# The expert stage of a hybrid decoder step: split products of 96 columns, or plain fp32 products in three 32-column groups

## The reference

```python
def swiglu(h, wg, wu, wd):
    return (jax.nn.silu(h @ wg) * (h @ wu)) @ wd

def moe_swiglu(h, router, wg, wu, wd):
    probs = jax.nn.softmax((h @ router).astype(F32), axis=-1)
    vals, idx = lax.top_k(probs, TOP_K)
    vals = vals / jnp.sum(vals, axis=-1, keepdims=True)
    combine = jnp.sum(jax.nn.one_hot(idx, N_EXPERTS, dtype=F32) * vals[..., None], axis=-2)
    out = jnp.zeros(h.shape, F32)
    for e in range(N_EXPERTS):
        out = out + combine[..., e:e + 1] * swiglu(h, wg[e], wu[e], wd[e]).astype(F32)
    return out.astype(h.dtype)
```

## Time and profile before

| | us |
|---|---|
| median of 3 runs | 1830.04 |
| lowest and highest of them | 1827.49, 1836.27 |
| the profiled execution's own time | 1834.22 |
| its span in the profile | 1832.1 |
| first product of the expert stage starts | 840.86 |
| last product of the expert stage ends | 1804.91 |

### The profile page before, as it was taken

One profiled execution on the slowest core, in us unless ns is written; L12 is line 12 of the kernel. 1 busy time (PEld: TensorE's weight loads), 2 busy tenths in 40 slices (PEclk: granted clock), 3 DMA queues, 4 the chain that ended last, 5 costly groups with the idle time before them and its releaser, 6 DMA issues.

```text
span 1832.1 us, 24602 instructions
## 1 busy us (share of the span) xinstructions
PE 1701.7 (93%) x9755; PEld 1365.5 (75%) x9755; DVE 1331.2 (73%) x1161; ACT 1079.6 (59%) x966; POOL 133.3 (7%) x132
## 2 busy tenths in 40 slices
PE   6999989899989966778999999999999999999994
PEld 6888769899989966676777777777777777777772
DVE  5556555455457689436888889888888888888885
ACT  4445543544445422336777777777777877877773
POOL 1022210000000464001000000000000000000001
PEclk9999999899999978788999999999999999999997
DMA  8588886355453552446999999999999999999962
GB/s 318 184 265 292 299 309 239 125 184 170 158 201 139 204 165 85 180 150 229 381 354 385 373 368 379 366 382 371 355 393 368 365 384 363 388 366 359 392 241 79
DMA packets 167969, 517.81 MB, mean 283 GB/s; under 512 B 6912, under 2 KB 58312, under 8 KB 160608
## 3 DMA queue, kind: packets, MB, share of 16 engines
q1 hardware_dynamic: 146144, 446.85, 65.8%
q0 software_dynamic: 16560, 60.99, 9.6%
q10 hardware_dynamic: 5200, 9.05, 1.4%
HBM read 475.97 MB, written 40.89 MB: 282 GB/s over the span
## 4 chain that ended last, share of the span: by engine, by line
PE 85%; DVE 6%; issue 2%; ACT 2%; DMA 1%; POOL 0%; POOLq 0%; ACTq 0%; DVEq 0%
PE ps L1663 82%; PE ps L2021 1%; DVE ring L1291 1%; DVE ring L1468 1%; PE ps L1805 1%; DVE ring L1469 1%; DMA ring<-in_state_retention 1%; PE ps L1971 0%; ACT ring_low_parts L931 0%; DVE arena L1486 0%; DVE ring L1442 0%; DMA ring<-y_scr,expert_arena 0%; PE ps L2007 0%; PE ps L1725 0%; DVE ring_low_parts L1240 0%
## 5 line engine op out<-in xcount | busy, mean ns | idle before, releaser
L1615 DVE TENSOR_TENSOR ring_low_parts<-ring,expert_weights_high 128x2048 fp32r<-128x2048 f32 x336 | 761.7, 2289 | 136.1 <-ACT expert_weights_high L1105 135.3
L1105 ACT CAST expert_weights_high<-ring 128x2048 fp32r<-128x2048 f32 x336 | 639.4, 1913 | 189.7 <-PE ps L1663 184.4
L1663 PE MATMUL ps<-expert_weights_high,expert_x_parts 128*96 128x512 f32 x1792 | 453.4, 395 | 3.8 <-ACT expert_weights_high L1105 3.8
L1663 PEld LDWEIGHTS ps<-expert_weights_high,expert_x_parts 128*96 128x96 f32 x1792 | 288.6, 162 | 126.2 <-ACT expert_weights_high L1105 3.9
L1240 DVE TENSOR_TENSOR ring_low_parts<-ring,ring_low_parts 128x1024 fp32r<-128x1024 f32 (+2 forms) x180 | 214.6, 1202 | 132.1 <-ACT ring_low_parts L931 130.9
L1663 PE MATMUL ps<-normed_high,ring_low_parts 128*128 128x264 f32 x1344 | 269.6, 292 | 9.7 <-DVE normed_low L1234 9.7
L931 ACT CAST ring_low_parts<-ring 128x1024 fp32r<-128x1024 f32 (+2 forms) x180 | 179.8, 1000 | 151.1 <-PE ps L1663 151.1
L1663 PE MATMUL ps<-ring_low_parts,expert_x_parts 128*96 128x512 f32 x896 | 243.9, 394 | 0.0
L1663 PEld LDWEIGHTS ps<-normed_high,ring_low_parts 128*128 128x128 f32 x1344 | 218.9, 192 | 12.1 <-issue 10.4
L1663 PE MATMUL ps<-expert_weights_high,hide_parts 128*96 128x512 f32 x896 | 226.2, 394 | 0.0
L1663 PEld LDWEIGHTS ps<-ring_low_parts,expert_x_parts 128*96 128x96 f32 x896 | 144.5, 161 | 63.2
(11 more groups left out here) (244 smaller groups left out, 1441.0 us busy)
## 6 DMA issues: line engine op xcount, KB each, us to landing
ring<-in_moe_w_gate SPq DMA_DIRECT2D x56, 2048.0 KB, 7.7
ring<-in_moe_w_up SPq DMA_DIRECT2D x56, 2048.0 KB, 8.0
ring<-in_moe_w_down SPq DMA_DIRECT2D x56, 2048.0 KB, 7.4
ring<-in_ret_w_in SPq DMA_DIRECT2D x8, 2048.0 KB, 12.1
ring<-in_state_retention POOLq DMA_DIRECT2D x32, 512.0 KB, 7.9
out_ret_s<-ring POOLq DMA_DIRECT2D x32, 512.0 KB, 5.0
ring<-in_hg_w_in SPq DMA_DIRECT2D x8, 2048.0 KB, 7.9
ring<-in_ffn_w_gate SPq DMA_DIRECT2D x11, 1024.0 KB, 5.4
```

Source lines behind the costliest of these rows:

```text
L1105: A.copy(half_hi(g), half_raw(g)).then_inc(w_hi_ok, 1)
L1615: V.tensor_tensor(half_lo(g), half_raw(g), half_hi(g).bitcast(F32), ALU.subtract)\
L1663: return nc.tensor.matmul(out, lhsT, rhs, start=first, stop=last)
```

## The change

The expert stage is written anew. Weights, x and hidden rows are multiplied in plain fp32, with no high and low parts. The 96 tokens are three groups of 32. A stationary operand is one group (128 by 32), and four products with different partition groups of PSUM stand in a row: for gate and up an item is one group of tokens by 512 features, 21 items, four to a bank, and the 21st is cut into four strided sets of 128 features. For down, each group of tokens has a bank, and its four partition groups are four blocks of 256 output columns.

A piece of gate or up is now one block of 128 input features by all 3584 (8 pieces of 1.8 MB), a piece of down 512 rows (7 pieces of 2 MB); one matrix fills the whole ring. The order of matrices is: gate of the first expert; then for each expert up, gate of the next expert, down. The hidden rows are turned in the middle of the next expert's gate, x of the next expert in the middle of up. ACT copies x, applies silu, copies turned rows and sums of down; DVE only multiplies silu of gate by up. The store of y is four transfers of 32 partitions in place of one of 96.

```diff
-EXPERT = (("g", 0, 0), ("g", 0, 1), ("u", 0, 0), ("u", 0, 1), ("g", 1, 0), ("g", 1, 1), ("u", 1, 0), ("u", 1, 1),
...
+GATE_BANKS = (6, 7, 0, 1, 2, 3)
+UP_BANKS = (0, 1, 2, 3, 4, 5)
+DOWN_BANKS = (4, 5, 6)
...
+            for k in range(KD):
+                sp.wait_ge(gate_used, k + 1)
+                load_k(moe_u, 0, k)
+
+            def visit(e, following, n):
+
+                for k in range(KD):
+                    sp.wait_ge(up_used, n * KD + (k + 1))
+                    load_k(moe_g, following, k)
+                sp.wait_ge(xg_full, n * 2 + 4)
+                load_rows(n + 3)
+                for q in range(QT):
+                    sp.wait_ge(gate_used, n * KD + (KD + last_k(q) + 1))
+                    load_q(e, q)
+                for k in range(KD):
+                    sp.wait_ge(down_used, n * QT + (last_q(k) + 1))
+                    load_k(moe_u, following, k)
...
+            with act.Fori(0, last) as n:
+                x_rows(n + 1)
+                act.wait_ge(up_used, n * KD + KD)
+                take_x(n + 1)
+                hidden_turned(n)
+                gate(n + 1)
+                store_y(n)
+            hidden_turned(last)
+            store_y(last)
...
-                        V.tensor_tensor(half_lo(g), half_raw(g), half_hi(g).bitcast(F32), ALU.subtract)\
-                            .then_inc(w_lo_ok, 1)
...
+                    V.tensor_tensor(hid_mem[:, c], hid_mem[:, c], ps[:, UP_BANKS[b], 0:c.stop - c.start], ALU.mult)\
+                        .then_inc(hid_ok2, 1)
...
-                            mm(o, x_hi[:, k, :], w, first and m < (1 if single else 2), False)
-                            mm(o, x_lo[:, k, :], w, False, False)
...
-                            i = mm(o, x_hi[:, k, :], w, False, last and m >= (3 if single else 2))
...
+            def wide(x, k, banks, ready, full, used):
+
+                w = k_piece(k)
+                for i in range(4 * WHOLE):
+                    if k == 0 and i % 4 == 0:
+                        ready(i // 4)
+                    q, g, z = i // GROUPS, i % GROUPS, 32 * (i % 4)
+                    j = mm(ps[z:z + 32, banks[i // 4], :], x[:, k, 32 * g:32 * g + 32], w[:, 512 * q:512 * q + 512],
+                           k == 0, k == KD - 1)
+                    if k == KD - 1 and i % 4 == 3:
+                        j.then_inc(full, 1)
+                if k == 0:
+                    ready(WHOLE)
+                for a in range(4):
+                    j = mm(ps[32 * a:32 * a + 32, banks[WHOLE], 0:P], x[:, k, C - 32:C], w[:, FE - 512 + a:FE:4],
+                           k == 0, k == KD - 1)
+                j.then_inc(used, 1)
...
+            def turn_hidden(n, b):
+
+                pe.wait_ge(hid_ok2, n * NBANK + (NBANK if b < 2 else b + 1))
+                if b >= 2:
+                    pe.wait_ge(t_ok, n * NBANK + (b - 1))
...
+            def down(n, arrival):
+                pe.wait_ge(t_ok, n * NBANK + NBANK)
+                for q in range(QT):
+                    pe.wait_ge(moe_arrived[q], arrival)
+                    for j in range(4):
+                        for g in range(GROUPS):
+                            i = GROUPS * q + g
+                            a = (4 * (i // 4) + j) * P + 32 * (i % 4) if i < 4 * WHOLE else WHOLE * 512 + 32 * j
+                            for c in range(4):
+                                m = mm(ps[32 * c:32 * c + 32, DOWN_BANKS[g], 0:256], hidT_mem[:, a:a + 32],
+                                       q_piece(q)[:, D * j + 256 * c:D * j + 256 * c + 256],
+                                       q + j == 0, q + j == QT + 2)
+                    m.then_inc(down_used, 1)
...
+            with pe.Fori(0, last) as n:
+                for k in range(KD):
+                    up(n, k)
+                    if k == 4:
+                        turn_rows(n + 1)
...
+                for k in range(KD):
+                    pe.wait_ge(moe_arrived[k], n * (48 if k < QT else 32) + 48)
+                    gate_piece(k, gate_ready)
+                    if 2 <= k < 5:
+                        turn_hidden(n, 2 * k - 4)
+                        turn_hidden(n, 2 * k - 3)
+                pe.wait_ge(gate_ok, n * NBANK + (NBANK + 1))
+                down(n, n * 48 + 64)
+            for k in range(KD):
+                up(last, k)
+            for b in range(NBANK):
+                turn_hidden(last, b)
+            down(last, last * 48 + 48)
```

More of the change, by code:

```diff
@@ L648, in hybrid_step, with k_piece, q_piece, last_q @@
         moe_u = ins["moe_w_up"][0].rearrange("e (k p) n -> p e k n", p=P)
[L650 to L699, removed]
+        moe_d = ins["moe_w_down"][0].rearrange("e (q p j) n -> p e q (j n)", p=P, j=4)
+        def k_piece(k):
+            return ring[:, KW * k:KW * k + KW]
+        def q_piece(q):
+            return ring[:, PIECE * q:PIECE * q + PIECE]
+        def last_q(k):
+            return (KW * k + KW - 1) // PIECE
+        def last_k(q):
+            return (PIECE * q + PIECE - 1) // KW
+        def item_columns(b):
+            return slice(512 * b, 512 * b + (512 if b < WHOLE else P))
         ret_in = ins["state_retention"][0].rearrange("b h (k p) e -> b h p k e", p=P)
@@ L769, in _ @@
+            with sp.Fori(0, NE - 1) as e:
+                visit(e, e + 1, e)
             sp.wait_ge(route_ok, 1)
@@ new lines, in gate, with hidden_turned @@
+            def gate(v):
+                for b in range(NBANK):
+                    if b < WHOLE:
+                        act.wait_ge(gate_full, v * WHOLE + (b + 1))
+                    else:
+                        act.wait_ge(gate_used, v * KD + KD)
+                    c = item_columns(b)
+                    A.activation(hid_mem[:, c], ps[:, GATE_BANKS[b], 0:c.stop - c.start], ACT.Silu).then_inc(gate_ok, 1)
+            def hidden_turned(n):
+                for b in range(NBANK):
+                    act.wait_ge(t_full, n * NBANK + (b + 1))
+                    c = item_columns(b)
+                    A.copy(hidT_mem[:, c], ps[:, 4 + b % 2, 0:c.stop - c.start]).then_inc(t_ok, 1)
@@ L1149, in _ @@
+            x_rows(0)
+            take_x(0)
+            act.sem_inc(y_store, 16)
+            act.sem_inc(y_free, 1)
+            gate(0)
+            with act.Fori(0, last) as n:
[7 more added lines that the diff above has]
+            store_y(last)
+            act.wait_ge(y_store, last * 64 + 80)
             A.copy(frs[:, 0:1], red3[:, 0:1]).then_inc(all_stored, 1)
@@ new lines, in _, with hidden @@
+            last = dve.value_load(nri[0:1, 1:2], min_val=NE - 1, max_val=ROUNDS * NE - 1)
+            def hidden(n):
+                for b in range(NBANK):
+                    c = item_columns(b)
+                    dve.wait_ge(gate_ok, n * NBANK + (b + 1))
+                    if b < WHOLE:
+                        dve.wait_ge(up_full, n * WHOLE + (b + 1))
+                    else:
+                        dve.wait_ge(up_used, n * KD + KD)
+                    V.tensor_tensor(hid_mem[:, c], hid_mem[:, c], ps[:, UP_BANKS[b], 0:c.stop - c.start], ALU.mult)\
+                        .then_inc(hid_ok2, 1)
@@ L1634, in _ @@
+            with dve.Fori(0, last) as n:
+                hidden(n)
+            hidden(last)
             for t in range(4):
```

315 lines of the change are left out of this document (109 added, 206 removed).

## The result

The changed kernel takes 1859.91 us (median of four runs, 1859.28 to 1861.4), the kernel before, on the same chip, 1830.8 (1827.49 to 1836.27). The ratio is 1.0157, with a 95% interval of 1.0131 to 1.0183. The forecast was 1775 us, faster.

A forecast was written before the change was run, and what follows sets the result against it. PE's own stream was taken as the bound: start 837.65 + 1.7 + 8 x 113.0 + 3.0 = 1746.4 for PE's end; with the tail and some 3 us of small waits, 1775 us. Range 1756 to 1814.

The forecast's parts named there:

- Sets side by side: Gate, up and down: four 32-column products run in parallel, 430 ns a set of 512 columns, 216 for 256; failure 0.02.
- The rival on weight loads: All 2880 sets: loads not covered in a long row, 25 ns a set giving 72 us, 1847; chance 0.11.
- The eight passes of the earlier trace: Retention stage: eight 128x512 passes with 32 columns over in 1.06 us, taken as evidence for parallel sets and covered loads.
- Period without the two faults: Expert stage: PE's work per expert forecast at 113.0 us, against 120.3 before.
- the going between 32-column and full products: Around four blocks of transposes per expert: 0.15 us for each of eight switches, 1.2 us.
- The strided item: Gate and up's 21st item: priced 2 x 0.11 us a piece; rival, each pass doubling, 28 us more, 1803, chance 0.08.
- PE's stream: Expert stage: PE's own stream is the bound, before and after the change; 1757 to 1790 us, chance 0.62.
- Start: Expert stage's first product: x needs one ACT copy per half and no weight split, so PE starts at about 837.65.
- The lower clock at the start: Expert stage's first eight products: 1.7 us at the lower clock, kept in the sum.
- The last expert's exposed turning: Hidden rows of the last expert, uncovered: 5 us less the 2.3 of transposes already counted, +3.0.
- Tail: After PE's end: copy, store, gather and norm stay; three more store issues add 0.8 us.
- Transfers: Weight loads: 110 us an expert taken, under PE's need; rival that they set the pace, 1783 to 1820, chance 0.13.

The follow-up runs named there:

- e2_tail: Changed kernel with the 21st item's four parts taking 128 neighbouring columns each in place of every fourth one: 1829.15 us, 0.9985 of before.
- e3_straight_mapping: Changed kernel with PE's seven passes through the expert loop written out and features in neighbouring blocks of 128 in all three matrices: 1786.7 us, 0.9751 of before.
- e9_pieces_after_router: e5_no_jump_left with SyncE waiting for the router's weights and final norm's gains before issuing the first expert's last four gate pieces: 1766.6 us, 0.964 of before.
- e7_body_smaller: Changed kernel, loop kept, down issuing 48 products of 336, so 461 calls to a body instead of 749: 1736.02 us, single run.
- e5_no_jump_left: e3_straight_mapping with the last expert's code directly behind the seventh body, the loop for further rounds behind it: 1777.55 us, 0.9695 of before.
- e4_short_body: Changed kernel, loop kept, down leaving out half of its products, so 585 calls to a body instead of 749: 1734.84 us, single run.
- e8_before_two_experts: Kernel before with two experts written out in one pass of TensorE's loop, four passes instead of eight: 1841.35 us, 1.0046 of before.

## Why the prediction was wrong

The sum at PE's end can be closed term by term. The forecast had 1746.4; the trace has 1829.1.

- **Sets side by side**, and loads covered: right. Down's 168 sets need (36.51 - 0.38) / 167 = 0.216 us each, 0.38 being a product's length; e2_tail's piece of 4.53 is 10 x 0.430 and two short passes of 0.115. The rival on weight loads falls: at 25 ns a set a piece would have taken 4.8 in e2_tail too. The Trainium skill's page "TensorE: Matmul & The Clock Gate", section "What overlaps and what doesn't", would have had every load standing open; in a row of 672 products on the same 128 rows none does. The eight passes of the earlier trace rows were a sound base.
- **Period without the two faults**: 112.5, forecast 113.0 (e3_straight_mapping). Eight times the difference: -3.8 us. The difference is the going between 32-column and full products, 1.2 us in the sum. Its sign is what the transposes take over the 3.2 counted for them (3.55 us) and the two pieces between them over the other pieces (4.65 each for 4.53), together 0.6 us for all eight changes.
- **The strided item**: mis-sized. The term was 2 x 0.11 a piece, and two strided passes take 0.47. The 113.0 priced the item at its bound from below. With the strided transposes it is 116.73 - 112.53 = 4.2 an expert, 33.6 in all. The rival had the mechanism and nearly the size (28). The chance was wrong: a bound for a form that no row shows should not have been the value taken, when the nearest strided row read 202 against 143. The Trainium skill's rule in "SBUF — State Buffer", section "Door 1: The DMA port swizzle", has the direction right, and the runs put the number to it: 0.12 us more for 128 columns 16 bytes apart.
- **The jump back**: the step that failed. "PE's stream" was taken to be its products, and where that stream comes from was not asked. Six gaps of 5.06 us on average with 3.2 of slow products and short stops behind: the period is (1698.76 - 1073.61) / 5 = 125.03 in the changed kernel and 116.73 without them, 8.3 x 6 = 49.8 us. No rival held it. It was to be foreseen in kind: the change doubled the code of the loop, and that the body of before ran without a fetch says nothing for one of twice its size. By itself this term turns the forecast around: 1775 + 50 = 1825, same.
- **Start**: 843.40 against 837.65, +5.8 us, and this is a difference of two terms. From the start of the turning of the tokens (`PE L1971` at 805.45 before, `PE L1933` at 802.03 in the changed kernel), the forecast left 32.2 us to the first product, and it took 41.4: +9.2, of which 5.6 are the wait and 3.4 the router's products at the lower clock. The turning itself began 3.4 us sooner in this execution; it begins anywhere from 798.7 to 805.5 us in the eleven profiled executions, and why stays open. The term counted the casts that go and forgot that the ring's four last gate pieces, of 1.8 MB each, now stand ahead of the router's weights. e9_pieces_after_router shows this cause: without it, 31.7 us lie between the two, and 32.2 were forecast.
- **The lower clock at the start** (1.7) did not come. The last expert's exposed turning took 5.4 us, where 2.3 + 3.0 were in the sum.
- **Tail**: 28.5 us from PE's end to the end of the span, 27.2 before, 0.8 expected on top.

1746.4 - 3.8 + 33.6 + 49.8 + 5.8 - 1.7 = 1830.1, 1.0 over the measured end.

**Transfers** were not the bound, as said: the rate that they allow, 108.9 us an expert in e7_body_smaller, is close to the 110 taken, and 3.6 under PE's 112.5. Whoever shortens PE's stream further meets them next.

## What to carry to other kernels

A loop on an engine has a size: when a change lengthens its body, look in the trace whether the instruction queue moves anything between the first pass and the last, and if it doesn't yet, price what happens when it does. Here, writing the loop out, with every path that isn't taken placed behind the one that is, was worth 48 us (38.7 and 9.2). An operand form that no row of the trace shows should enter the sum at the dearer of its bounds, or be changed into one that it shows. And a small load that an engine waits for has to be issued before the large ones, not beside them: the wait in the chain is called by its name, but what has to move is what was queued ahead of it.

## What the hardware showed

- The size of code can be read from straight code: in e5_no_jump_left the instruction queue moved 1.08 MB from 1000 to 1650 us, which is 650 / 112.5 experts of 749 calls, so 250 bytes a call. The changed kernel's body has 187 KB by that, e4_short_body's 146 and e7_body_smaller's 115, a little under what its expectation said; all three fetch all through, and PE stands idle 4.3 to 5.9, 4.9 to 5.4 and 3.7 to 4.2 us at each jump (in the last, up's weights land only some 0.6 to 0.9 us into it). The body of the kernel before has at most 92 KB (0.49 MB for 650 / 122 experts in e8_before_two_experts) and ran eight times without a pause, with no fetch behind the first pass, in which five packets of 16 KB came. Where between 92 and 115 the bound lies was not narrowed.
- Straight code is also fetched all the time and never stops PE. A jump forward over a body costs as much as a jump back: 5.79 and 1.97 us.
- A pause of 4.4 us was followed by 4 us at a granted clock of 0.50; one of 2.5 by 4 us at 0.60.
- A plain fp32 product with 128 moving columns 16 bytes apart lasts 400 ns, with neighbouring ones 273.
- With 16 engines full of 14 KB packets (share 1.00, 423 to 431 GB/s), a load of 32 KB took 11.2 to 11.6 us to land; with four pieces fewer ahead of it, 2.2. In the kernel before, the engines were as full (1.02, 411 GB/s, packets of 4 KB) and it took 3.9: whether the bytes queued ahead or the size of their packets decides was not tried.
